# First attention of a two-layer fp32 kernel: one merged score block per head instead of two

## The chip, the cores and the metric

One Trainium2 chip, one of its cores. The metric is device time in microseconds of one execution. Everything is fp32; most matrix products are made of three passes over a high and a low part (hi*hi, hi*lo, lo*hi).

## What is computed

Two transformer mixers follow each other on a sequence of 512 tokens of width 2048. The change lies in the first one, a sliding-window attention with 32 query heads of 64, 4 key/value heads (groups of 8 query heads), a T5 bias and a sink per head:

```python
def swa_sink_mixer(h, w_in, q_gain, k_gain, sinks, rel_table, w_out):
    q, k, v, gate = jnp.split(h @ w_in, [...], axis=-1)          # L = SWA_BLOCK = SWA_WINDOW = 128
    q = rms_norm(q.reshape(bsz, seq, SWA_KV_HEADS, SWA_GROUP, SWA_HEAD_DIM), q_gain)
    k = rms_norm(...); v = ...; k_pad, v_pad = jnp.pad(k, pad), jnp.pad(v, pad)
    dist = qi + L - kj                                           # qi: 0..127, kj: 0..255
    in_band = (dist >= 0) & (dist < SWA_WINDOW)
    def one_block(args):                                         # a block of 128 queries
        s = jnp.einsum('bqhgd,bkhd->bhgqk', qj, kb) * scale + bias
        s = jnp.where(in_band & (start - L + kj >= 0), s, -jnp.inf)
        m = jnp.maximum(jnp.max(s, axis=-1, keepdims=True), sink)
        p = jnp.exp(s - m)
        p = p / (jnp.sum(p, axis=-1, keepdims=True) + jnp.exp(sink - m))
        return jnp.einsum('bhgqk,bkhd->bqhgd', p, vb)
    return (o * jax.nn.silu(gate)) @ w_out
```

A query of a block sees 128 keys out of 256: in the block before its own those with a column above its own, in its own block those up to it. So each of the 128 columns is allowed in exactly one of the two blocks.

## The kernel before, in words

There is no scheduler: each engine's program is written out, and semaphores order them. The first attention runs inside the projections of the first layer. For each key/value head `g` (four) there are 32 half steps `H`. In each, TensorE issues six 512-column matmuls of a projection (two of four token tiles; `project` L744 to L746, or `project_gate` L760 to L762 for the last `g`), and between them pieces of the attention of group `g`. Two half steps use up one k tile of weights, which ScalarE splits into a high part (`make_hi` L1360) and GpSimd into a low part (`make_lo` L1988), three tiles ahead of TensorE, once in every even half step.

The attention of a group has 16 units `u` (4 pairs of heads `hp` by 4 query blocks `j`; n counts over all groups). For unit `u`:

- half step u + 11, TensorE `scores` (L864, L865): for both heads of the pair 128 queries against 256 keys (128 for j = 0), into one PSUM bank per head. It waits for `s_m`, VectorE's signal that it has read the unit before.
- VectorE `soften` in the same half step: copies the sink (L2253), then for each head one custom instruction (L2256) that reads the scores from PSUM, adds the bias, negates, writes `sm` and keeps the extreme value.
- u + 12, ScalarE `weigh` (L1468): the exponential with its sum, 257 columns a head, into `p_w`.
- u + 13, VectorE `denominators` (L2263, L2266): reciprocal, then the rescaling of `p_w`, 512 columns (256 for j = 0). In VectorE's program it stands ahead of the `soften` of that half step.
- u + 14, TensorE `turn_p` (L878): transposes the weights, four 128 x 128 blocks (two for j = 0), after the scores of that half step. ScalarE `keep_pT` (L1478) copies them to SBUF.
- H = 18, 22, 26, 30, TensorE `values` (L891): the product of a pair with `vg`, eight matmuls, between that half step's scores and transposes; VectorE `keep_o` (L2270) copies the result.

ScalarE's order in a half step is `weigh`, the copies of the turned queries, `keep_pT`, and in an even one the weight split. Queries and keys are turned in half steps 3 and 6 to 9 (L853).

Of the kernel before, what the change touches and what calls it, by code (L numbers as in the profile page):

```python
# [127 lines left out]
def build(nc, a, out):  # L128
    with ExitStack() as ctx:
# [30 lines left out]
        p_w = over("p_w", [P, 3, 2, 256 + 1], B_HI + 8192)  # L160
        sm = over("sm", [P, 2, 2, 256 + 1], B_HI + 14368)
# [3 lines left out]
        kT_lo = over("kT_lo", [P, S], B_HI + 28736, F32R)  # L165
        o_T = over("o_T", [P, KC, S], B_LO)
# [18 lines left out]
        den = sb("den", [P, 2, 2])  # L185
# [9 lines left out]
        pT, P_W = place("pT", [P, 2, NT * 256])  # L195
# [150 lines left out]
        s_scaled_p, s_r_row = sem("s_scaled_p"), sem("s_r_row")  # L346
# [210 lines left out]
        def meta_window(unit):  # L557

            return metaT[:, unit:unit + FULL // META].rearrange("p a b -> p (a b)")

# [160 lines left out]
        def _(pe):  # L721
# [113 lines left out]
            for k in range(KC):  # L835
                for t in range(NT):
                    project(1, k, t, setA_hi, setA_lo)
                if k == 12:
                    pe.wait_ge(s_r_row, 1)
                    for t in range(NT):  # L840
                        last = mm(turn[0][:, t * P:(t + 1) * P], ones[:], r_diag[:, t], start=True, stop=True)
                    last.then_inc(s_r_row, 1)

            def q_turn(g, b):

                if b == 0:
                    pe.wait_ge(s_kdup, g + 1)
                else:
# [7 lines left out]
            def scores(g, u):  # L856
# [3 lines left out]
                pe.wait_ge(s_m, g * UNITS + u + EARLY)  # L860
# [7 lines left out]
            def turn_p(g, u):  # L868
# [5 lines left out]
                else:  # L874
                    pe.wait_ge(s_pT, g * UNITS + u)
# [465 lines left out]
        def _(act):  # L1341
# [111 lines left out]
            for k in range(KC):  # L1453
                split_hi(1, k)
                if k == 13:
                    act.wait_ge(s_r_row, 2)
                    nc.scalar.activation(r_row[:], turn[0][:], ACT.Copy).then_inc(s_r_row, 1)
# [3 lines left out]
            def weigh(g, u):  # L1461

                n = g * UNITS + u
                act.wait_ge(s_m, n + 1 + EARLY)
                act.wait_ge(s_tr, n)
                first = P if u % NT == 0 else 0
                for h in range(2):
                    last = nc.scalar.activation(p_w[:, n % 3, h, first:], sm[:, u % 2, h, first:], ACT.Exp,  # L1468
                                                bias=negm[:, u % 2, h:h + 1], scale=-1.0, accum_out=den[:, u % 2, h:h + 1])
                last.then_inc(s_p, 1)  # L1470

            def keep_pT(g, u):
                act.wait_ge(s_tr, g * UNITS + u + 1 + EARLY)
                j = u % NT
                if j == 0:
                    act.wait_ge(s_pv, 4 * g + u // NT + EARLY)
                first = P if j == 0 else 0
                nc.scalar.activation(pT[:, :, j * 256 - P + first:j * 256 + P],  # L1478
                                     turn[0][:].rearrange("p (h k) -> p h k", h=2)[:, :, first:256], ACT.Copy).then_inc(s_pT, 1)
# [12 lines left out]
            for g in range(4):  # L1492
                for H in range(32):
# [12 lines left out]
                    if 0 <= H - 14 < UNITS:  # L1506
                        keep_pT(g, H - 14)
                    if H % 2 == 0:
# [473 lines left out]
        def _(pool):  # L1982
# [50 lines left out]
            root(r_x[:], ss_x[:], NT, ROOT_X)  # L2033
            for k in range(KC):
# [147 lines left out]
        def _(dve):  # L2182
# [32 lines left out]
            last.then_inc(s_r_row, 1)  # L2215
# [31 lines left out]
            def soften(g, u):  # L2247
# [4 lines left out]
                hp, first = u // NT, P if u % NT == 0 else 0  # L2252
                V.tensor_copy(sm[:, u % 2, :, 256:257], sink_g[:, 2 * hp:2 * hp + 2].unsqueeze(2))  # L2253
# [698 lines left out]
```

## Time and profile before

| | |
|---|---|
| median of 3 runs | 1585.67 us (1583.68 to 1586.33) |
| profiled execution | 1584.18 us |
| its span | 1582.3 us |
| TensorE busy | 1569.8 us (99%) |
| VectorE, ScalarE, GpSimd busy | 889.5, 811.2, 675.0 us |
| first attention, from its first turn of keys | 101 us to 363 us |

The span is the time between the first and the last instruction of the program. A matmul's busy time begins with its issue and overlaps that of the next, so the distance between starts tells what one costs TensorE. A long duration of an instruction on VectorE or GpSimd can contain a wait that no semaphore shows.

### The profile page before, as it was taken

To read this page: it belongs to the slowest core of one execution; us is meant where nothing else is said; L and a number is where in the kernel's file an instruction comes from. 1 tells how busy PE (TensorE), PEld (TensorE's weight loads), DVE (VectorE), ACT (ScalarE), POOL (GpSimd) and SP (SyncE) were. 2 spreads that over 40 slices of the span, in tenths; PEclk is the share of its full clock that TensorE was granted. 3 is DMA by queue.
4 is the path that set the end of the run, shared out by engine and by line. 5 is a ranking of instruction groups with operands and counts; after the bars stand their busy time and mean duration, and the time that the engine had idled before them with its cause. 6 is when DMAs were issued, how large, how long until landed. Compare 5 with 4: busy or idle time off the path is not lost.

```text
span 1582.3 us, 22135 instructions
## 1 busy us (share of the span) xinstructions
PE 1569.8 (99%) x8143; PEld 1276.7 (81%) x8143; DVE 889.5 (56%) x1846; ACT 811.2 (51%) x1695; POOL 675.0 (43%) x569
## 2 busy tenths in 40 slices
PE   9999999999999999999999999999999999999998
PEld 7788888888888888887777787888887888888886
DVE  4257757674357876468554532423255454876675
ACT  5456776764334455454444365444466665344561
POOL 5543433436766304575111034544444426664022
PEclk9999999999999999999999999999999999999999
DMA  9554655656887878858999858545554325625762
GB/s 345 146 166 94 163 122 156 161 119 149 192 203 182 241 238 271 222 192 176 258 274 292 198 184 284 168 133 142 160 158 128 114 68 143 151 80 159 241 239 106
DMA packets 139383, 285.41 MB, mean 180 GB/s; under 512 B 11227, under 2 KB 17820, under 8 KB 138604
## 3 DMA queue, kind: packets, MB, share of 16 engines
q1 hardware_dynamic: 85660, 164.49, 31.3%
q0 software_dynamic: 31664, 81.70, 25.1%
q10 hardware_dynamic: 21952, 37.81, 7.6%
q8 instruction: 65, 1.06, 0.3%
q14 instruction: 42, 0.34, 0.1%
HBM read 259.01 MB, written 92.06 MB: 222 GB/s over the span
## 4 chain that ended last, share of the span: by engine, by line
PE 91%; DMA 3%; POOL 2%; ACT 1%; issue 1%; DVE 1%; SPq 0%; POOLq 0%; DVEq 0%
PE acc L744 14%; PE acc L746 14%; PE acc L745 14%; PE acc L760 3%; PE acc L762 3%; PE acc L761 3%; PE turn L1237 3%; PE acc L926 2%; PE acc L927 2%; PE acc L928 2%; PE sc L926 2%; PE turn L926 2%; PE sc L928 2%; PE sc L927 2%; PE turn L927 2%; PE turn L928 2%
## 5 line engine op out<-in xcount | busy, mean ns | idle before, releaser
L1988 POOL TENSOR_TENSOR w_lo<-w_raw,w_hi 128x512 fp32r<-128x512 f32 x341 | 510.1, 1505 | 651.7 <-ACT w_hi L1360 650.8
L1360 ACT ACTIVATE w_hi<-w_raw 128x512 fp32r<-128x512 f32 x565 | 354.1, 629 | 445.5 <-PE acc L746 174.1
L744 PE MATMUL acc<-w_hi,setA_hi 128*128 128x512 f32 (+1 forms) x820 | 331.2, 404 | 0.9 <-ACT stage L1374 0.5
L746 PE MATMUL acc<-w_hi,setA_lo 128*128 128x512 f32 (+1 forms) x820 | 315.9, 385 | 0.0
L745 PE MATMUL acc<-w_lo,setA_hi 128*128 128x512 f32 (+1 forms) x820 | 314.8, 384 | 0.0
L2413 DVE TENSOR_TENSOR w_lo<-w_raw,w_hi 128x512 fp32r<-128x512 f32 x224 | 156.2, 703 | 134.7 <-ACT w_hi L1360 134.0
L746 PEld LDWEIGHTS acc<-w_hi,setA_lo 128*128 128x128 f32 x820 | 153.9, 188 | 31.5
L744 PEld LDWEIGHTS acc<-w_hi,setA_hi 128*128 128x128 f32 x820 | 154.4, 188 | 29.5 <-issue 4.9
L745 PEld LDWEIGHTS acc<-w_lo,setA_hi 128*128 128x128 f32 x820 | 154.7, 189 | 24.1
L760 PE MATMUL acc<-setA_hi,w_hi 128*128 128x512 f32 x256 | 101.9, 398 | 0.0
L762 PE MATMUL acc<-setA_lo,w_hi 128*128 128x512 f32 x256 | 99.9, 390 | 0.0
L761 PE MATMUL acc<-setA_hi,w_lo 128*128 128x512 f32 x256 | 99.7, 389 | 0.0
L744 PE MATMUL acc<-w_hi,setB_hi 128*128 128x512 f32 x192 | 76.5, 398 | 0.3 <-POOL w_lo L1988 0.3
L746 PE MATMUL acc<-w_hi,setB_lo 128*128 128x512 f32 x192 | 75.0, 390 | 0.0
L745 PE MATMUL acc<-w_lo,setB_hi 128*128 128x512 f32 x192 | 74.8, 390 | 0.0
L1468 ACT ACTIVATE p_w<-sm,negm 128x257 f32<-128x257 f32 (+1 forms) x128 | 60.5, 475 | 21.7 <-DVE negm L2256 21.5
L1817 ACT ACTIVATE p<-sm,negm 128x144 f32<-128x144 f32 (+3 forms) x96 | 54.5, 569 | 30.5 <-DVE negm L2731 18.6
L1478 ACT ACTIVATE pT<-turn 128x256 f32<-128x256 f32 (+1 forms) x64 | 34.9, 545 | 42.9 <-PE turn L878 42.8
L762 PEld LDWEIGHTS acc<-setA_lo,w_hi 128*128 128x128 f32 x256 | 48.0, 188 | 10.3
L760 PEld LDWEIGHTS acc<-setA_hi,w_hi 128*128 128x128 f32 x256 | 48.1, 188 | 9.6 <-issue 0.5
L761 PEld LDWEIGHTS acc<-setA_hi,w_lo 128*128 128x128 f32 x256 | 48.1, 188 | 9.1
L2256 DVE CUSTOM_DVE_ANT_0 sm<-sc,bias,sink_g 128x256 f32<-128x256 f32 (+1 forms) x128 | 52.1, 444 | 0.1
(552 smaller groups left out, 3192.0 us busy)
## 6 DMA issues: line engine op xcount, KB each, us to landing
w_raw<-in_swa_w_in SPq DMA_DIRECT2D x35, 1024.0 KB, 7.6
w_raw<-in_w_in SPq DMA_DIRECT2D x32, 1024.0 KB, 5.6
w_raw<-sum_out SPq DMA_DIRECT2D x64, 256.0 KB, 4.5
sum_k<-in_w_in POOLq DMA_DIRECT2D x24, 512.0 KB, 6.6
sum_out<-in_swa_w_out POOLq DMA_DIRECT2D x24, 512.0 KB, 7.5
sum_v<-in_w_in POOLq DMA_DIRECT2D x24, 512.0 KB, 8.7
w_raw<-in_w_in SPq DMA_DIRECT2D x48, 256.0 KB, 5.5
sum_out<-in_w_out POOLq DMA_DIRECT2D x24, 512.0 KB, 6.8
```

The costliest lines, as they stand in the source:

```text
L744: mm(acc[t][:, 0:cols], hi[:, kc, rows], wh, start=(k == 0), stop=False)
L745: mm(acc[t][:, 0:cols], hi[:, kc, rows], wl, start=False, stop=False)
L746: last = mm(acc[t][:, 0:cols], lo[:, kc, rows], wh, start=False, stop=(k == K - 1))
L760: mm(acc[t][:], wh, setA_hi[:, k], start=(k == 0), stop=False)
L761: mm(acc[t][:], wl, setA_hi[:, k], start=False, stop=False)
L762: last = mm(acc[t][:], wh, setA_lo[:, k], start=False, stop=(k == KC - 1))
L926: mm(dst, hi, wh, start=start, stop=False)
L927: mm(dst, hi, wl, start=False, stop=False)
L928: last = mm(dst, lo, wh, start=False, stop=stop)
L1360: nc.scalar.activation(w_at(f)[0], raw_of(f), ACT.Copy).then_inc(done, 1)
L1988: nc.gpsimd.tensor_tensor(lo, raw_of(f), hi.bitcast(F32), ALU.subtract).then_inc(s_lo, 1)
L2413: V.tensor_tensor(lo, raw_of(f), hi.bitcast(F32), ALU.subtract).then_inc(s_wlo, 1)
```

## The change

The two score blocks of a head are merged after the bias: VectorE takes the smaller of the two halves (both are negated, and a banned entry is 1e30), so that exponentials, rescaling, transposes and their copies are 128 columns a head in every unit. In the product, all weights are multiplied with the values of the own block, and those that belong to the block before (columns above the diagonal, `pT_before`, a product with the mask `above`) once more with `v_step`, the difference of the values of the two blocks. The sink copy is made only for the units that begin a buffer's use in a pair (`u % 4 < 2`). `s_m` now counts twice for a unit with j > 0: after the read, which `scores` waits for, and after the `min`, which `weigh` waits for; `softened` and `befores` are these counts. VectorE's `soften` stands ahead of `denominators`, `keep_before` behind it, and `keep_o` is ScalarE's. The semaphore of `r_row` is merged into another.

```diff
+        v_step = over("v_step", [P, NT - 1, HD], B_HI + 30784)
+        def softened(units):
+            return EARLY + 2 * units - (units + NT - 1) // NT
...
             def scores(g, u):
-                pe.wait_ge(s_m, g * UNITS + u + EARLY)
+                n = g * UNITS + u
+                pe.wait_ge(s_m, softened(n - 1) + 1 if n > 0 else EARLY)
...
             def turn_p(g, u):
                 for h in range(2):
-                    for c in range(1 if j == 0 else 0, 2):
-                        last = nc.tensor.transpose(turn[0][:, (2 * h + c) * P:(2 * h + c + 1) * P],
-                                                   p_w[:, n % 3, h, c * P:(c + 1) * P], ident[:])
+                    last = nc.tensor.transpose(turn[0][:, h * P:(h + 1) * P], p_w[:, n % 3, h, 0:P], ident[:])
...
             def values(g, hp):
+                pe.wait_ge(s_before, befores(g * UNITS + (hp + 1) * NT))
-                for c in (0, 2, 1, 3):
-                    keys, end = slice(c * 256, min(c * 256 + 256, 7 * P)), min(c * P + 256, S)
+                for b in range(NT):
                     for h in range(2):
-                        last = mm(o_ps[h * HD:(h + 1) * HD, c * P:end], vg[:, c], pT[:, h, keys],
-                                  start=(c == 0), stop=(c == 3))
+                        last = mm(o_ps[h * HD:(h + 1) * HD, b * P:(b + 1) * P], vg[:, b], pT[:, h, b * P:(b + 1) * P],
+                                  start=(b == 0), stop=False)
+                for b in range(1, NT):
+                    for h in range(2):
+                        last = mm(o_ps[h * HD:(h + 1) * HD, b * P:(b + 1) * P], v_step[:, b - 1], pT_before[:, h, b * P:(b + 1) * P],
+                                  start=False, stop=(b == NT - 1))
...
             def weigh(g, u):
-                act.wait_ge(s_m, n + 1 + EARLY)
+                act.wait_ge(s_m, softened(n + 1))
-                    last = nc.scalar.activation(p_w[:, n % 3, h, first:], sm[:, u % 2, h, first:], ACT.Exp,
+                    last = nc.scalar.activation(p_w[:, n % 3, h], sm[:, u % 2, h], ACT.Exp,
...
+            def keep_o(g, hp):
+                act.wait_ge(s_pv, 4 * g + hp + 1 + EARLY)
+                nc.scalar.activation(o_T[:, 4 * g + hp], o_ps[:], ACT.Copy).then_inc(s_o, 1)
...
             def soften(g, u):
+                if n >= 2:
+                    dve.wait_ge(s_p, n - 1)
+                if n > 0:
+                    dve.wait_ge(s_m, softened(n))
+                if u % NT < 2:
+                    V.tensor_copy(sm[:, u % 2, :, P:P + 1], sink_g[:, 2 * hp:2 * hp + 2].unsqueeze(2))
                 for h in range(2):
                     head = 2 * hp + h
-                    last = V.tensor_tensor_reduce(sm[:, u % 2, h, first:256], sc[h][:, first:256],
+                    dst = s_both[:, h] if first == 0 else sm[:, u % 2, h, 0:P]
+                    last = V.tensor_tensor_reduce(dst, sc[h][:, first:256],
                                                   bias[:, head, first:], -1.0, sink_g[:, head:head + 1],
                                                   ALU.add, ALU.min, negm[:, u % 2, h:h + 1])
                 last.then_inc(s_m, 1)
+                if first == 0:
+                    dve.wait_ge(s_m, softened(n) + 1)
+                    V.tensor_tensor(sm[:, u % 2, :, 0:P], s_both[:, :, 0:P], s_both[:, :, P:256], ALU.min).then_inc(s_m, 1)
...
             def denominators(g, u):
+                rows = p_w[:, (g * UNITS + u) % 3, :, 0:P]
+                V.tensor_tensor(rows, rows, rden[:, u % 2].unsqueeze(2).to_broadcast([P, 2, P]), ALU.mult).then_inc(s_scaled_p, 1)
+            def keep_before(g, u):
+                dve.wait_ge(s_pT, g * UNITS + u + 1)
+                V.tensor_tensor(pT_before[:, :, j * P:(j + 1) * P], pT[:, :, j * P:(j + 1) * P],
+                                above[:].unsqueeze(1).to_broadcast([P, 2, P]), ALU.mult).then_inc(s_before, 1)
...
+                    if 0 <= H - 11 < UNITS:
+                        soften(g, H - 11)
                     if 0 <= H - 13 < UNITS:
                         denominators(g, H - 13)
-                    if 0 <= H - 11 < UNITS:
-                        soften(g, H - 11)
+                    if 0 <= H - 14 < UNITS:
+                        keep_before(g, H - 14)
```

VectorE, half step 16 (scores of unit 5 in `sc`, weights of unit 3 in `p_w`) of a group; ISA is the custom instruction that reads the scores, shown for the first of two heads. Before:

```order
L2263 RECIPROCAL rden<-den 128x2 [waits s_p]
L2266 TENSOR_TENSOR p_w<-p_w,rden 128x2x256 [waits s_d]
L2253 COPY sm<-sink_g 128x2 [waits s_score]
L2256 ISA sm,negm<-sc,bias,sink_g 128x256
L2256 ISA negm 128x1
```

Now:

```order
L2282 COPY sm<-sink_g 128x2 [waits s_m,s_p,s_score]
L2286 ISA s_both,negm<-sc,bias,sink_g 128x256
L2286 ISA negm 128x1
L2292 TENSOR_TENSOR sm<-s_both 128x2x128 [waits s_m]
L2296 RECIPROCAL rden<-den 128x2 [waits s_p]
L2298 TENSOR_TENSOR p_w<-p_w,rden 128x2x128 [waits s_d]
L2307 TENSOR_TENSOR pT_before<-pT,above 128x2x128 [waits s_pT]
```

The rescaling (into `p_w`), which the transposes of the next half step wait for, stood ahead of the reads of the scores; now the two reads and the `min` are ahead of it, and the masked copy (`pT_before`) is behind it.

TensorE, half step 18: transposes of half step 17, then scores of unit 7 and values. Before:

```order
L878 MATMUL turn<-ident,p_w 128x128 [waits s_pT,s_scaled_p]
L878 MATMUL turn<-ident,p_w 128x128 x3
L744 MATMUL acc<-w_hi,setA_hi 128x512 [waits s_lo]
L864 MATMUL sc<-kT_hi,qT_a 128x256 [waits s_m]
L891 MATMUL turn<-pT,vg 64x256 [waits s_o,s_qT,s_pT]
L891 MATMUL turn<-pT,vg 64x256 x5
L891 MATMUL turn<-pT,vg 64x128 x2
```

Now:

```order
L891 MATMUL turn<-ident,p_w 128x128 [waits s_pT,s_scaled_p]
L891 MATMUL turn<-ident,p_w 128x128
L756 MATMUL acc<-w_hi,setA_hi 128x512 [waits s_lo]
L878 MATMUL sc<-kT_hi,qT_a 128x256 [waits s_m]
L903 MATMUL turn<-pT,vg 64x128 [waits s_qT,s_o,s_before,s_pT]
L903 MATMUL turn<-pT,vg 64x128 x7
L907 MATMUL turn<-pT_before,v_step 64x128 x6
```

The transposes are two instead of four, the values fourteen matmuls instead of eight, and their wait has `s_before`, VectorE's masked copy, beside ScalarE's copy.

## Rows read from the trace of the kernel before

**Rows 1.** Busy time and share on the page; engine, us, records.
```profile
PE 1569.8 (99%) x8143; PEld 1276.7 (81%) x8143; DVE 889.5 (56%) x1846; ACT 811.2 (51%) x1695; POOL 675.0 (43%) x569
```

**Rows 2.** All waits of TensorE, first and last of eight: total, times, longest.
```profile
PE sc L808 <- POOL half L2026: 1.7, 1, 1.7
...
PE acc L744 <- POOL w_lo L1988: 0.3, 1, 0.3
```

**Rows 3.** Busy time of each engine in one group of the first attention, 101.14 to 168.38.
```profile
101.14:168.38 67.24, 67.24 (x398) 55.22 (x397) 46.61 (x142) 46.13 (x120) 26.70 (x24) 1.00 0.59 141
```

**Rows 4.** Timeline of TensorE, 187.1 to 196.8 us (start, length).
```profile
187.18 0.28 PE L864 MATMUL sc<-kT_hi,qT_a 128*128 128x256 f32 x1
...
187.66 0.38 PE L878 MATMUL turn<-ident,p_w 128*128 128x128 f32 x2
189.26 0.22 PE L864 MATMUL sc<-kT_hi,qT_a 128*128 128x128 f32 x1
...
191.50 0.28 PE L864 MATMUL sc<-kT_hi,qT_a 128*128 128x256 f32 x1
...
191.85 0.28 PE L865 MATMUL sc<-kT_lo,qT_a 128*128 128x256 f32 x1
191.97 0.60 PE L878 MATMUL turn<-ident,p_w 128*128 128x128 f32 x4
193.78 0.28 PE L864 MATMUL sc<-kT_hi,qT_a 128*128 128x256 f32 x1
...
196.07 0.29 PE L864 MATMUL sc<-kT_hi,qT_a 128*128 128x256 f32 x1
...
196.65 0.44 PE L891 MATMUL turn<-pT,vg 128*64 128x256 f32 x2
```

**Rows 5.** Busy time of L891 alone (records) in two stretches of one product.
```profile
263.93:265.27 1.34, 1.34 (x12) 0.92 (x14) 1.00 0.83 289
265.28:265.55 0.27, 0.27 (x6) 0.14 (x2) 1.00 1.11 417
```

**Rows 6.** Timeline of VectorE after the scores of 191.50 us.
```profile
192.17 0.17 DVE L2253 COPY sm<-sink_g 128x2 f32<-128x2 f32 x1
192.25 0.48 DVE L2256 CUSTOM_DVE_ANT_0 sm<-sc,bias,sink_g 128x256 f32<-128x256 f32 x1
...
193.05 0.17 DVE L2263 RECIPROCAL rden<-den 128x2 f32<-128x2 f32 x1
193.25 0.43 DVE L2266 TENSOR_TENSOR p_w<-p_w,rden 128x256 f32<-128x256 f32 x1
```

**Rows 7.** Weight loads of the transposes (source view): ns min/median/max.
```profile
L878 PEld LDWEIGHTS turn<-ident,p_w x224: 137/140/145, 120.3 to 359.9; 128*128 128x128 f32 x112
```

**Rows 8.** Timeline of ScalarE, 188.1 to 191.8 us.
```profile
188.16 0.39 ACT L1478 ACTIVATE pT<-turn 128x256 f32<-128x256 f32 x1
188.44 0.62 ACT L1360 ACTIVATE w_hi<-w_raw 128x512 fp32r<-128x512 f32 x1
...
191.37 0.41 ACT L1468 ACTIVATE p_w<-sm,negm 128x129 f32<-128x129 f32 x1 [0.46 <-DVE negm L2256]
```

**Rows 9.** Timelines of VectorE and GpSimd, 184.5 to 190.8 us.
```profile
184.55 1.29 POOL L1988 TENSOR_TENSOR w_lo<-w_raw,w_hi 128x512 fp32r<-128x512 f32 x1 [2.21 <-ACT w_hi L1360]
185.22 0.91 DVE L2266 TENSOR_TENSOR p_w<-p_w,rden 128x256 f32<-128x256 f32 x1
...
188.94 0.69 DVE L2266 TENSOR_TENSOR p_w<-p_w,rden 128x512 f32<-128x512 f32 x1
189.14 1.64 POOL L1988 TENSOR_TENSOR w_lo<-w_raw,w_hi 128x512 fp32r<-128x512 f32 x1 [3.30 <-ACT w_hi L1360]
189.85 0.95 DVE L2253 COPY sm<-sink_g 128x2 f32<-128x2 f32 x1 [0.22 <-PE sc L865]
```

**Rows 10.** VectorE by shape, 100 to 370 us: busy us, mean ns.
```profile
L2256 DVE CUSTOM_DVE_ANT_0 sm<-sc,bias,sink_g 128x256 f32<-128x256 f32 x96 | 42.3, 478 | 0.0
...
L2266 DVE TENSOR_TENSOR p_w<-p_w,rden 128x256 f32<-128x256 f32 x16 | 8.8, 548 | 0.5
```

More of the change, by code:

```diff
@@ L158, in build @@
         bias = over("bias", [P, GROUP, 256], B_HI)
-        p_w = over("p_w", [P, 3, 2, 256 + 1], B_HI + 8192)
-        sm = over("sm", [P, 2, 2, 256 + 1], B_HI + 14368)
+        p_w = over("p_w", [P, 3, 2, P + 1], B_HI + 8192)
+        s_both = over("s_both", [P, 2, 256], B_HI + 11328)
+        above = over("above", [P, P], B_HI + 32128)
+        sm = over("sm", [P, 2, 2, P + 1], B_HI + 14368)
         qT_a = over("qT_a", [P, GROUP // 2, S], B_HI + 18496, F32R)
@@ L559, in meta_window, with befores @@
             return metaT[:, unit:unit + FULL // META].rearrange("p a b -> p (a b)")
+        def softened(units):
+            return EARLY + 2 * units - (units + NT - 1) // NT
+        def befores(units):
+            return (NT - 1) * (units // NT) + max(units % NT - 1, 0)
         def head_T(b, h):
@@ L838, in _ @@
                 if k == 12:
-                    pe.wait_ge(s_r_row, 1)
+                    pe.wait_ge(s_rel, 2)
                     for t in range(NT):
                         last = mm(turn[0][:, t * P:(t + 1) * P], ones[:], r_diag[:, t], start=True, stop=True)
-                    last.then_inc(s_r_row, 1)
+                    last.then_inc(s_rel, 1)
             def q_turn(g, b):
@@ L1455, in _ @@
                 if k == 13:
-                    act.wait_ge(s_r_row, 2)
-                    nc.scalar.activation(r_row[:], turn[0][:], ACT.Copy).then_inc(s_r_row, 1)
+                    act.wait_ge(s_rel, 3)
+                    nc.scalar.activation(r_row[:], turn[0][:], ACT.Copy).then_inc(s_rel, 1)
             act.wait_ge(s_kn, 2)
@@ L1507, in _ @@
                         keep_pT(g, H - 14)
+                    if H >= 18 and (H - 18) % NT == 0:
+                        keep_o(g, (H - 18) // NT)
                     if H % 2 == 0:
@@ L2033, in _ @@
             root(r_x[:], ss_x[:], NT, ROOT_X)
+            nc.gpsimd.memset(above[:], 1.0).then_inc(s_ident, 1)
+            pool.wait_ge(s_ident, 4)
+            nc.gpsimd.affine_select(out=above[:], in_=above[:], compare_op=ALU.is_gt, fill=0.0, base=0,
+                                    pattern=[[-1, P]], channel_multiplier=1).then_inc(s_ident, 1)
             for k in range(KC):
@@ L2214, in _ @@
                 last = V.tensor_scalar(r_diag[:, t], ident[:], r_x[:, t:t + 1], None, ALU.mult)
-            last.then_inc(s_r_row, 1)
+            last.then_inc(s_rel, 1)
             dve.wait_ge(s_small, 80)
@@ L2259, in soften @@
                 last.then_inc(s_m, 1)
+                if first == 0:
+                    dve.wait_ge(s_m, softened(n) + 1)
+                    V.tensor_tensor(sm[:, u % 2, :, 0:P], s_both[:, :, 0:P], s_both[:, :, P:256], ALU.min).then_inc(s_m, 1)
             def denominators(g, u):
                 dve.wait_ge(s_p, g * UNITS + u + 1)
[L2263 to L2270 removed]
+                after(dve, V.reciprocal(rden[:, u % 2], den[:, (g * UNITS + u) % 3]))
+                rows = p_w[:, (g * UNITS + u) % 3, :, 0:P]
+                V.tensor_tensor(rows, rows, rden[:, u % 2].unsqueeze(2).to_broadcast([P, 2, P]), ALU.mult).then_inc(s_scaled_p, 1)
+            def keep_before(g, u):
+                j = u % NT
+                if j == 0:
+                    return
+                if j == 1:
+                    dve.wait_ge(s_pv, 4 * g + u // NT + EARLY)
+                dve.wait_ge(s_pT, g * UNITS + u + 1)
+                V.tensor_tensor(pT_before[:, :, j * P:(j + 1) * P], pT[:, :, j * P:(j + 1) * P],
+                                above[:].unsqueeze(1).to_broadcast([P, 2, P]), ALU.mult).then_inc(s_before, 1)
             def keep_gate(c):
```

36 lines of the change are left out of this document (15 added, 21 removed).

## The prediction

> **What bounds the kernel now.** I read the page's busy shares first: TensorE is busy 99% of a 1582.3 us span [rows 1]. Then the waits of TensorE: the longest is 1.7 us at the start, the shortest listed 0.3 us, none of the eight lies in the first attention, and together they are under 5 us [rows 2]. So time here is the sum of what TensorE issues, and a gain must come from it. The table by stage shows the same for one key/value group of the first attention (32 half steps, 67.24 us): TensorE 67.24 us busy, VectorE 46.6, ScalarE 46.1, GpSimd 26.7, granted clock 1.00 (the 2.4 GHz level) [rows 3]. Four groups are four such stretches. VectorE has 20.6 us to spare per group, but it is not evenly spread: with scores and transposes in flight, a half step is 2.28 us long, and in it VectorE works some 1.8 (192.17 to 193.25, and 0.69) [rows 6, 9].
>
> The lengths of half steps come from the timeline of TensorE [rows 4]. Scores to scores is 2.08 us (187.18 to 189.26) where the half step turns two blocks (first block of a pair), and 2.28 and 2.29 us (191.50, 193.78, 196.07) where it turns four. The distance from the transposes' start to the next scores is 1.60 us (187.66 to 189.26) against 1.81 us (191.97 to 193.78).
>
> **The sum, TensorE.** *Transposes.* In 48 of 64 units two of four transposes go: 2.28 or 2.29 less 2.08 is 0.21 us a unit, 48 x 0.21 = 10.1 us. The four records of a unit span 0.60 us and one takes 0.27, so they follow each other every 0.11 us [rows 4]: 96 x 0.11 = 10.6 us is the other bound. I take **-10.2**. The Trainium skill, page "TensorE: Matmul & The Clock Gate", section "Back-to-back issue gap", gives some 81 ns for a 128-column matmul with its weight load in a sustained stream; by it the 96 would be worth only 7.8 us, an estimate. The row measures the fp32 transposes of this kernel, so it decides.
>
> *Values.* Eight matmuls (six of 256 columns, two of 128) become fourteen of 128: 1792 columns either way. The six wide ones (12 records) take 1.34 us, 0.22 each; the two narrow ones take 0.27 us or a little less to the last start, 0.11 to 0.13 each [rows 5]. 14 x 0.11 = 1.54 against 1.56; the six more issues cost at most their own 0.11 each, 0.66 a pair, were they not shorter. I take **+0.5** for all 16 pairs (0 to 10).
>
> **VectorE.** Per unit behind the first block it gains the `min` of two halves (256 elements) and `keep_before` (256), the rescaling shrinks from 512 to 256; the copy of o (0.69 us, 16 times) leaves for ScalarE; half of the sink copies go. The nearest row for each 256-element operation with both inputs in SBUF is the old rescaling of a first block, 0.43 us undisturbed [rows 6]. Counted at the distance to the next start, 0.36, that is 12 x 0.72 more, 12 x 0.27 and 4 x 0.6 less: some +2.5 us in a group. On the average that fits. It is the order that doesn't.
>
> Take t = 0 at the scores of unit 5 (half step 16; it turns unit 2). Last score at 0.64 (191.50 to 191.85 + 0.28) [rows 4], VectorE's sink copy from 0.67, its two reads from 0.75 at 0.40 each (192.25 to 193.05), the last maximum out at 1.64 [rows 6]. The new `min` must wait for VectorE's own signal, 1.67 to 2.10; reciprocal from 2.03, rescaling of unit 3 from 2.23. Before, that rescaling stood *ahead* of the reads. TensorE wants it for the transposes of unit 3 at 2.08 + 0.47 = 2.55. Undisturbed it is there at 2.66 and, with a weight load of 0.14 [rows 7], the transposes start at 2.80: 0.25 late.
>
> It will not be undisturbed. ScalarE copies unit 2's transposes from 0.88 (0.85 their last result, as 187.66 + 0.38), begins the weight tile's high part 0.28 later and needs 0.62, and GpSimd starts its low part 0.08 after that [rows 8]: at 1.86, inside the `min`. What happens then, two pairs of rows show [rows 9]. GpSimd's 1.29 us subtraction, begun at 189.14 while the rescaling ran (188.94 to 189.63), took 1.64: it ran from 0.14 before that ended. A 256-element rescaling begun at 185.22 under GpSimd's (184.55 to 185.84) ended at 186.13, 0.29 after it: 0.91 instead of 0.43. The groups by shape agree: 16 such rescalings have a mean of 548, while the reads of PSUM stay at 478 [rows 10]. So the two engines exclude each other where VectorE reads SBUF twice. The Trainium skill says so too ("SBUF — State Buffer", "Who interferes with whom": the loser waits for the whole instruction), and it speaks against this change, which gives VectorE two such operations more per unit.
>
> Hence GpSimd gets through at 2.10 - 0.14 = 1.96 and ends at 3.25; the rescaling ends at 3.54, the transposes start at 3.68 instead of 2.55: **1.13 us of stall**. GpSimd's window to do so reaches from the reads to 2.23, so its start may be 0.3 later or much earlier. VectorE is now late: `keep_before` of unit 2 from 3.47, reads of unit 6 from 3.83 to 4.72, `min` to 5.18, rescaling to 5.74, `keep_before` of unit 3 to 6.10. TensorE: scores of unit 7 at 3.68 + 1.60 = 5.28, values 0.58 later (196.07 to 196.65) at 5.86 [rows 4], but they need unit 3's masked part: 6.10 + 0.14 = 6.24, **0.38 us**. During the values (1.6 us) VectorE catches up. This is 1.51 us for each pair whose values run among scores: three of four.
>
> Two smaller ones per group. Before the first transposes half steps are 2.08 - 0.21 = 1.87 long; unit 0's rescaling follows unit 2's `min` and ends at 2.58, usable at 2.72, wanted at 2.34: 0.38, with the low part of half step 12 about **0.45**. And after a values step ScalarE copies o before it splits the weights, so that GpSimd's operation starts with the scores of units 8 and 12 and holds the sink copy (0.95 instead of 0.17 in such a case [rows 9]); the next scores are late by about **0.25**, twice. A group: 3 x 1.51 + 0.45 + 0.5 = 5.5; four: **+21.9**. ScalarE's own changes (exponentials 0.41 instead of 0.50 twice a unit [rows 8], copies halved, 0.6 for o) leave it lighter. "Banks freed at the read" frees nothing earlier: the old signal too came with the second read; it only keeps the `min` out of that wait. The mask, the difference of v and the merged semaphores are issued once, or once a group outside the scores, and I put them at nothing; their cover is the lead of three weight tiles, and gone it would cost under 1 us.
>
> Sum: -10.2 + 0.5 + 21.9 = +12.2, rounded to **+12**. The profiled execution took 1584.18 us for its span of 1582.3, so 1596.2 for one like it; against the median of 1585.67 this is 1597.5. Bounds: if the new operations ran at 0.36 a piece, VectorE would be 0.2 us a unit quicker and the stall about 17, +7; if GpSimd comes after the rescaling and holds `keep_before` instead, reads, the next scores and the values are late, about 0.8 + 0.9 a pair, which with slower `min`s of 0.5 makes +16 to +18.
>
> **The rivals.** *A, all of it hidden* (faster): VectorE is 69% busy in the stage, and stalls are absorbed because its engine runs ahead between pairs. Place: the transposes; price: none; it decides if the rescaling lands before 2.41, that is if `min` and its wait cost under 0.2 us together. Then only -10.2 + 0.5: 1576. For it: not one wait of TensorE today [rows 2]. Against it: the operation of this size takes 0.43 [rows 6]. The skill's "Perfetto Trace Analysis", section "Identifying the Most-Contended Engine", would have one cut the busiest engine first, and by occupancy that is TensorE; that rule gives this rival's time. *B, no collision with GpSimd* (no change): the order stalls of 0.25 at the transposes remain, and reckoned on as above 0.40 at the values, 0.65 a pair, with 0.45 a group: 2.4 a group, 9.6 in all, net -0.1: 1585.6. It decides if GpSimd asks outside of 0.75 to 2.23. *C, heavier* (slower): +16 to +18, 1603.
>
> **How the numbers follow.** Forecast 0.62, C 0.08, a milder stall (+4 to +8) 0.04, B 0.15, A 0.11. Slower by over 0.2% (3.2 us, about what a measurement of this kernel can tell from no change) is 0.74; B spreads over both sides of none, 0.11 within 0.2% and 0.04 beyond; so faster is 0.15. The range takes C and B in and leaves A out: 1582 to 1604; the forecast's own is 1592 to 1602.
>
> **What would show it.** Right: in the first attention TensorE waits for VectorE, the longest total before the transposes (`turn`) about 1 us a time, released by the rescaling, 12 times; a second group before the values released by the masked copy, 12 times of some 0.4; 256-element rescalings of over 1 us; a group of about 70 us instead of 67.24, with TensorE busy some 64.7 of it. Wrong: groups of 64.7 us and no such waits (A), or waits of 0.2 to 0.4 alone (B); a values step longer by over 0.1; or a difference outside the first attention, where nothing should move.

## The result, and the profile after

| | before | after |
|---|---|---|
| median on the same chip | 1584.76 us (4 runs) | 1599.7 us (4 runs) |
| profiled span | 1582.3 us | 1597.6 us |
| second group of the first attention, k turn to k turn | 67.25 us | 71.09 us |

The changed kernel is slower: ratio 1.0093, 95% interval 1.0075 to 1.011, that is some 14.7 us. The forecast was 1597.5 with a range of 1582 to 1604. The granted clock was 1.00 in both throughout the first attention. A k turn is the first transpose of a group's keys; from one to the next is a group. Ratios, here and below, are of fast executions alone; one of the eight of the kernel with the paced low part took 5306 us and is not among them.

The page's busy line [rows 1] and TensorE's waits [rows 2] of the changed kernel, matmuls (PE) first, then weight loads (PEld); columns: total us, times, longest:

```profile
PE 1569.3 (98%) x8239; PEld 1275.5 (80%) x8239; DVE 903.5 (57%) x1898; ACT 799.4 (50%) x1711; POOL 676.4 (42%) x571
...
PE turn L891 <- DVE p_w L2298: 11.2, 16, 0.9
PE turn L903 <- issue: 2.7, 12, 0.2
...
PE turn L866 <- DVE kT_lo L2264: 1.1, 3, 0.4
PE acc L756 <- ACT stage L1390: 1.0, 3, 0.4
...
PEld turn L891 <- DVE p_w L2298: 14.5, 16, 1.1
...
PEld turn L903 <- issue: 6.3, 16, 0.4
```

TensorE is as busy as before, 1569.3 against 1569.8 us, in a span 15.3 us longer. It has 96 fewer transposes, and 96 more records all the same, because the values of a pair leave 28 records where they left 16. It now waits 16 times at the transposes (L891) for the rescaling (L2298): 12 times at units 3, 7 and 11 of a group and 4 times at unit 0. It waits 12 times or more at the values (L903), three times at the k/q turns (L866) and three times at the first matmul of a projection, twice at L756 and once at L772. (The third wait in the row of L756, 0.4 us, lies outside the first attention; the kernel before has one like it.) The prediction has neither the waits at the k/q turns nor those at the first matmuls.

The second group, as [rows 3] for the first (us, then busy us and records of PE, PEld, DVE, ACT, POOL, clock, DMA share, GB/s):

```profile
173.00:244.10 71.10, 66.94 (x422) 54.54 (x421) 51.22 (x157) 42.90 (x123) 26.71 (x24) 1.00 0.56 133
```

TensorE was busy in all 67.24 us of a group; now it is busy 66.94 of 71.10, so that 4.2 us are seen as idle. The stalls are longer than that, 6.4 us in the list below, because busy time covers a part of each: a score matmul is recorded as 0.28 us long where the next usually starts 0.12 behind it, so the first 0.16 us of a wait counts as busy, and the pair of transposes behind a stall is itself recorded as longer (0.44 against 0.38).

The turn of unit 3 in the changed kernel, from the timeline of all engines; it answers to [rows 6, 9]:

```profile
198.26 0.62 ACT L1376 ACTIVATE w_hi<-w_raw 128x512 fp32r<-128x512 f32 x1
...
198.76 0.42 DVE L2292 TENSOR_TENSOR sm<-s_both 128x256 f32<-128x256 f32 x1
...
198.96 1.36 POOL L2008 TENSOR_TENSOR w_lo<-w_raw,w_hi 128x512 fp32r<-128x512 f32 x1 [1.81 <-ACT w_hi L1376]
199.10 0.15 DVE L2296 RECIPROCAL rden<-den 128x2 f32<-128x2 f32 x1
...
199.29 1.31 DVE L2298 TENSOR_TENSOR p_w<-p_w,rden 128x256 f32<-128x256 f32 x1
...
199.51 0.28 PE L879 MATMUL sc<-kT_lo,qT_a 128*128 128x256 f32 x1
...
200.53 0.41 DVE L2307 TENSOR_TENSOR pT_before<-pT,above 128x256 f32<-128x256 f32 x1
200.66 0.20 PEld L891 LDWEIGHTS turn<-ident,p_w 128*128 128x128 f32 x2 [1.07 <-DVE p_w L2298]
200.66 0.44 PE L891 MATMUL turn<-ident,p_w 128*128 128x128 f32 x2 [0.87 <-DVE p_w L2298]
```

GpSimd asks at 198.96, inside the `min` (198.76 to 199.18), and is let in. It ends at 200.32. The rescaling, issued at 199.29, ends at 200.60: 0.28 after GpSimd, where undisturbed it takes 0.43. The transposes start 1.15 us after the last score matmul; undisturbed the distance is 0.12 (191.85 to 191.97 [rows 4]). The reciprocal of two numbers ran in between at its usual length.

I laid the starts of TensorE's matmuls side by side for the two kernels, without those of transposes and values. The distance between the traces grows by 14.1 us over the first attention, from 1.3 to 15.4, lies between 14.0 and 15.4 afterwards and ends at 15.3. In the second group it changes in these places: each unit behind the first of a pair takes 0.19 to 0.24 less; units 3, 7 and 11 bring 1.06 to 1.09 of stall each (1.04 to 1.10 in all four groups); each of their values 0.31; unit 0's transposes 0.47, and the scores of unit 3 ahead of them 0.16; the scores of units 9 and 13 0.29 and 0.26; the next projection's first two matmuls 0.53, and the q turn of half step 6 0.55. The last two come three times each, for there are three next projections.

### The profile page after: what moved, and what is told of

Same layout as the page of the kernel before. It is cut to its first block, busy times and chain, and to the rows that moved or that the text cites. A ratio compares the mean times of both kernels' runs of the same rounds, so it can differ in the third digit from the quotient of the medians.

```text
span 1597.6 us, 22483 instructions
## 1 busy us (share of the span) xinstructions
PE 1569.3 (98%) x8239; PEld 1275.5 (80%) x8239; DVE 903.5 (57%) x1898; ACT 799.4 (50%) x1711; POOL 676.4 (42%) x571
## 4 chain that ended last, share of the span: by engine, by line
PE 85%; DVE 6%; DMA 3%; ACT 2%; POOL 2%; issue 2%; SPq 0%; ACTq 0%; DVEq 0%; POOLq 0%
PE acc L756 14%; PE acc L758 13%; PE acc L757 13%; PE acc L772 3%; PE acc L774 3%; PE acc L773 3%; PE turn L1253 3%; PE acc L942 2%; PE acc L943 2%; PE acc L944 2%; PE sc L942 2%; PE turn L942 2%; PE sc L943 2%; PE sc L944 2%; PE turn L944 2%; PE turn L943 2%
## 5 line engine op out<-in xcount | busy, mean ns | idle before, releaser
L756 PE MATMUL acc<-w_hi,setA_hi 128*128 128x512 f32 (+1 forms) x820 | 331.2, 404 | 1.2 <-ACT stage L1390 1.0
L756 PEld LDWEIGHTS acc<-w_hi,setA_hi 128*128 128x128 f32 x820 | 154.3, 188 | 29.8 <-issue 5.8
L772 PE MATMUL acc<-setA_hi,w_hi 128*128 128x512 f32 x256 | 101.8, 398 | 0.3 <-ACT stage L1390 0.3
L756 PE MATMUL acc<-w_hi,setB_hi 128*128 128x512 f32 x192 | 76.2, 397 | 0.0
L1483 ACT ACTIVATE p_w<-sm,negm 128x129 f32<-128x129 f32 x128 | 50.4, 397 | 40.1 <-DVE sm L2292 21.9
L772 PEld LDWEIGHTS acc<-setA_hi,w_hi 128*128 128x128 f32 x256 | 48.1, 188 | 10.0 <-issue 0.9
L2766 DVE MEMSET tick<- 128x1 f32 x96 | 5.7, 59 | 81.1 <-PE sc L1192 67.0
L1253 PE MATMUL turn<-nat_v,pT 128*128 128x128 f32 x320 | 48.8, 283 | 0.4
```

The costliest lines, as they stand in the source:

```text
L756: mm(acc[t][:, 0:cols], hi[:, kc, rows], wh, start=(k == 0), stop=False)
L772: mm(acc[t][:], wh, setA_hi[:, k], start=(k == 0), stop=False)
L1253: mm(dst, pT2[:, u % 2, b * P:(b + 1) * P], nat_v[:, buf, b], start=(b == 0), stop=False)
```

## The experiments

Two claims were open. **One:** the loss is the order of VectorE's queue together with GpSimd's exclusion. **Two,** found in the comparison: 1.07 us a group comes from the output copy on ScalarE. (The expectations split this as 0.45 at the matmul and 0.62 at the turn; by the steps above it is 0.53 and 0.55.) All ratios are to the kernel before, on the same chip. "Group" is the distance from the second to the third k turn (67.25 before, 71.09 after); four times its change is the steadiest measure, for single executions differ by 1.4 us before the attention begins (below); it takes four times what comes three times only.

| kernel | ratio, 95% interval | group, us |
|---|---|---|
| changed kernel | 1.0093, 1.0075 to 1.011 | 71.09 |
| output copy on VectorE | 1.006, 1.0048 to 1.0072 | 69.44 |
| low part paced | 1.0037, 1.0023 to 1.0051 | 69.22 |
| both | 1.0005, 0.9996 to 1.0014 | 67.43 |
| no low parts | 0.9988, 0.9979 to 0.9996 | 67.02 |
| no masked product | 1.0058, 1.0044 to 1.0072 | 70.22 |
| rescaling first | 1.007, 1.0057 to 1.0082 | 70.31 |
| min last, copy on VectorE | 1.005, 1.0038 to 1.0063 | 69.18 |
| the same, low part paced | 0.9969, 0.9958 to 0.9981 | 65.91 |
| before, copy on ScalarE | 1.002, 1.0011 to 1.0028 | 68.49 |
| before, reads first | 1.0006, 0.9997 to 1.0015 | 67.55 |
| before, low part paced | 1.001, 1.0001 to 1.0018 | 67.43 |

**The low part paced.**

```diff
                     if H % 2 == 0:
+                        if H >= 14:
+                            pool.wait_ge(s_scaled_p, g * UNITS + min(H - 13, UNITS - 1) + 1)
                         split_lo(2 + g, H // 2)
```

> The changed kernel with one wait added on GpSimd: from half step 14 on, its low part of the weights starts only after the rescaling of the same half step. Theory one (GpSimd gets the shared access at the end of the min, holds it for its 1.3 us, and the rescaling waits for it): the stalls at the turns of units 3, 7 and 11, 12 of about 1.1 us, fall to 0.3 or less each; the values wait may grow by 0.2 each, since the masked product now meets the low part. Time falls by 9 us (6 to 12) against the changed kernel, to about 1590. Rival (VectorE is late through the order and the amount of its own work; GpSimd is not in it): the stalls stay near 1.1 us, the time within 2 us of the changed kernel, or slower, since weights come up to 3 us later.

Measured: 1.0037 against 1.0093, 8.9 us less. Nothing but GpSimd's start was moved. TensorE's waits in 90 to 315 us (three groups' turns):

```profile
PE turn L903 <- issue: 3.5, 9, 0.4
PE turn L891 <- DVE p_w L2300: 0.8, 3, 0.3
...
PEld turn L903 <- issue: 6.2, 12, 0.6
...
PEld turn L891 <- DVE p_w L2300: 2.9, 12, 0.5
```

The 1.1 us stalls at the turns are gone. What is left there is unit 0, as before, and 0.12 us at each of units 3, 7 and 11: their transposes start 0.24 behind the last score matmul instead of 0.12. The values wait longer: they start 0.67 behind the last score matmul where it was 0.51, and their weight loads wait up to 0.6 us where it was 0.4. That is not mainly for the reason I gave: the low part now meets the next unit's `min` (mean 515 ns against 472; the masked product 446 against 430), and the masked product stands behind that. The rival falls.

**No low parts at all.**

```diff
-                        split_lo(2 + g, H // 2)
+                        f = B[2 + g] + H // 2 + AHEAD
+                        pool.wait_ge(s_hi, number[f] + 1)
+                        nc.gpsimd.memset(w_at(f)[1].bitcast(F32), 0.0).then_inc(s_lo, 1)
```

> The changed kernel with GpSimd's subtraction for the low parts of the weights in the four projections beside the first attention replaced by a write of zeros of the same size at the same place in its queue: the low parts of these weights are left out of the computation, the matmuls on them stay. Theory one (two engines exclude each other while GpSimd reads and writes for 1.3 us): VectorE's rescalings of over 1 us are gone, the turn stalls fall from about 1.1 to 0.2 us, time 10 to 14 us under the changed kernel, unless a pure write excludes as well; then each is as long as the write, and the gain is 1.3 minus that length, times 12. Rival (VectorE's own order): no change within 2 us.

Measured: 0.9988, 16.6 us less than the changed kernel, above the 10 to 14 expected. In the second group the turns of units 3, 7 and 11 give back 0.87 each. The rest comes from other places: unit 0's transposes 0.13, the scores of units 3, 9 and 13 0.17, 0.29 and 0.25, and the q turn of half step 6 0.53. The values still start 0.50 behind the last score matmul. This kernel still has the copy on ScalarE, and is already 0.1% ahead of before. So the stalls at the scores of units 9 and 13 and at that q turn need GpSimd's subtraction as well as the copy: at the q turn VectorE's four scalings of q take 2.50 us together beside the write and 3.59 beside the subtraction. Only the 0.53 at the next projection stays here, and comes from the copy alone. VectorE and GpSimd by shape, 100 to 370 us (busy us, mean ns, idle before):

```profile
L2300 DVE TENSOR_TENSOR p_w<-p_w,rden 128x256 f32<-128x256 f32 x64 | 27.3, 426 | 2.2
L2294 DVE TENSOR_TENSOR sm<-s_both 128x256 f32<-128x256 f32 x48 | 20.4, 425 | 1.7
...
L2068 POOL MEMSET w_lo<- 128x512 f32 x63 | 33.2, 526 | 211.0 <-ACT w_hi L1376 211.0
```

and one such step from its timeline:

```profile
194.60 0.42 DVE L2294 TENSOR_TENSOR sm<-s_both 128x256 f32<-128x256 f32 x1
...
194.78 0.53 POOL L2068 MEMSET w_lo<- 128x512 f32 x1 [2.69 <-ACT w_hi L1376]
...
195.13 0.42 DVE L2300 TENSOR_TENSOR p_w<-p_w,rden 128x256 f32<-128x256 f32 x1
```

The write from 194.78 to 195.31 lies over the end of the `min` and the start of the rescaling, and neither is longer for it. In the changed kernel the same two groups are:

```profile
L2298 DVE TENSOR_TENSOR p_w<-p_w,rden 128x256 f32<-128x256 f32 x61 | 36.6, 600 | 2.1
L2292 DVE TENSOR_TENSOR sm<-s_both 128x256 f32<-128x256 f32 x48 | 22.7, 472 | 1.7
```

**The output copy back on VectorE.**

The call leaves ScalarE's loop and stands at the end of VectorE's half step:

```diff
-                act.wait_ge(s_pv, 4 * g + hp + 1 + EARLY)
-                nc.scalar.activation(o_T[:, 4 * g + hp], o_ps[:], ACT.Copy).then_inc(s_o, 1)
...
+                dve.wait_ge(s_pv, 4 * g + hp + 1 + EARLY)
+                V.tensor_copy(o_T[:, 4 * g + hp], o_ps[:]).then_inc(s_o, 1)
```

> The changed kernel with the copy of the output (keep_o) back on VectorE, at the end of its half step as before; all else of the change stays. Laid side by side, the traces of before and after show 1.07 us in each of the first three groups that no term of the forecast holds: 0.45 at the first matmul of the next projection and 0.62 at the q turns of half step 6. Theory one (the copy on ScalarE waits for the values, and the evacuation of the next projection's banks stands behind it in ScalarE's queue): both go, and the time falls by about 3.2 us (2 to 4.5) against the changed kernel, with the 12 stalls of about 1.1 us at the turns of units 3, 7 and 11 unchanged. Rival (they come from VectorE's own added work at the head of a group, the differences of the values, or from nothing that this copy touches): no change within 1 us, or up to 3 us slower, because VectorE gets 16 copies of 0.69 us (row of before) back.

Measured: 1.006, 5.2 us less than the changed kernel, where 3.2 (2 to 4.5) was expected. The turn stalls are as they were (11.0 us, 12 times, longest 1.1, at the weight loads in 90 to 315 us), the waits at L866 for `kT_lo` and at L756 for `stage` are gone, and so are those of the scores of units 9 and 13: 0.25 to 0.29 twice a group, 2.1 us in four. These the prediction has as a term that comes from this very copy, and I left them out of what I expected here. 3.2 + 2.1 is 5.3. ScalarE's timeline at the end of a projection, changed kernel:

```profile
162.54 0.38 ACT L1492 ACTIVATE pT<-turn 128x256 f32<-128x256 f32 x1 [0.71 <-PE turn L891]
165.60 0.60 ACT L1497 ACTIVATE o_T<-turn 128x512 f32<-128x512 f32 x1 [2.68 <-PE turn L907]
166.09 0.62 ACT L1376 ACTIVATE w_hi<-w_raw 128x512 fp32r<-128x512 f32 x1
166.62 2.42 ACT L1390 ACTIVATE stage<-acc,r_x 128x512 f32<-128x512 f32 x4
```

and with the copy on VectorE:

```profile
160.86 0.39 ACT L1492 ACTIVATE pT<-turn 128x256 f32<-128x256 f32 x1 [0.71 <-PE turn L891]
161.14 0.62 ACT L1376 ACTIVATE w_hi<-w_raw 128x512 fp32r<-128x512 f32 x1
161.67 1.28 ACT L1390 ACTIVATE stage<-acc,r_x 128x512 f32<-128x512 f32 x2
```

ScalarE stood idle for 2.68 us in front of `o_T`, waiting for the values, with the weight split and the evacuation behind it in its queue. From the last copy of `pT` to the evacuation it is 4.08 us in the one and 0.81 in the other.

**The same part alone, in the kernel before.** Edit: `keep_o` taken from VectorE and put behind `keep_pT` on ScalarE.

> The kernel before with one part of the change alone: the copy of the output moved from VectorE to ScalarE, behind the copy of the turned scores. Theory one (it delays the evacuation of the next projection by waiting for the values): 1 us in each of the first three groups, so +3 us (1.5 to 4.5), in the gaps at the first matmul of each projection and at the q turns. Rival (before, ScalarE's queue had other slack and VectorE gains 16 times 0.69 us): within 1 us of before, or up to 4 us faster.

Measured: 1.002 (1.0011 to 1.0028), +3.2 us, though VectorE is 9 us less busy (880.1 against 889.5). The group is 1.24 us longer, and the same two steps are in it, 0.54 at the next projection and 0.52 at the q turn. Theory two holds in both directions.

**Both repairs together.**

> The changed kernel with both repairs and its order kept (score reads, min, rescaling, masked product): the output copy on VectorE, and GpSimd's low part behind the rescaling of its half step from half step 14 on. By themselves they gave back about 5.2 and 8.9 us of the 14.7. Theory one (two separate causes, so they add, and little else is lost): 1.000 to 1.002 times before, 1586 to 1588, with the change's own gain of some 10 us still eaten by waits at the values (the masked product now meets the low part) and at each group's first turn. Rival (they overlap, or one hides the other): the ratio stays at 1.003 or above; or, if GpSimd was all, the order is nothing and it comes to 0.997, as with the min last.

Measured: 1.0005, 13.9 us less than the changed kernel, where 5.2 and 8.9 add to 14.1. The two repairs add. (They touch different stalls, since the pacing begins at half step 14 and does nothing at the q turn of half step 6.) What eats the rest of the gain stands in the waits (90 to 315 us):

```profile
PE turn L903 <- issue: 3.5, 9, 0.4
PE turn L891 <- DVE p_w L2294: 0.8, 3, 0.3
PEld turn L903 <- issue: 6.1, 12, 0.6
PEld turn L891 <- DVE p_w L2294: 3.0, 12, 0.5
```

**The masked product left out.** Edit: no `keep_before`, no wait for it, and the second part of the values reads `pT`.

> The changed kernel without the masked product: VectorE's 48 of 0.42 us a piece and the values' wait for them are left out, and the second part of the values multiplies the unmasked scores, so the causal part of the output is not computed. Theory one (it sits behind the rescaling at the end of VectorE's queue and delays only the values of its half step): the turn stalls stay at 12 times 1.1 us, the values' stall of about 0.4 us goes where it was not the matmuls' own start, so 1.5 to 5 us less than the changed kernel, 1594 to 1598. Rival (VectorE's amount of work is what counts, so 20 us less of it frees the turns too): 10 us less or more.

Measured: 1.0058, 5.5 us less by the two ratios (2 to 9 with their intervals) and 3.5 us by the group, 4 x 0.87. The turn stalls stay, 10.9 us in 12 weight loads, longest 1.1, as in the changed kernel. So 48 operations fewer on VectorE, 20 us of its work, don't touch the turns; the amount of its work is not the cause. 0.87 over three values is 0.29 each, which is the values' wait: they start 0.21 us behind the last score matmul here, as before the change, against 0.51 in the changed kernel. The profile itself puts the waits at L903 down to "issue" and doesn't name the masked product; this run does.

**VectorE's old order in the merged kernel.** Edit: `denominators` ahead of `soften`.

> The changed kernel with VectorE's order as before: the rescaling (denominators) ahead of the score reads and the min, all else of the change kept. Theory one (VectorE's queue in a half step is what TensorE waits for, so order only chooses who waits): the 1.1 us at the turns of units 3, 7 and 11 go, and waits come at the scores of units 3, 5 and 7, for the reads now stand behind the rescaling and the low part that may be in front of it: 0.4 to 0.8 us each; against the changed kernel 0 to 4 us less, 1596 to 1600. Rival (reads first is the cause of the loss; the merged form would do well in the old order): 8 us or more less, to 1591 or under.

Measured: 1.007, 3.6 us less than the changed kernel. The stalls moved from the turns to the scores: 0.3 us each at units 3 and 5, and 0.8 each at units 7, 11 and 15, of which I had named only 7 (90 to 315 us):

```profile
PE sc L878 <- DVE negm L2286: 6.1, 12, 0.6
...
PEld sc L878 <- DVE negm L2286: 15.5, 21, 1.1
```

**The kernel before with reads first.** Edit: `soften` ahead of `denominators`, a third slot of `den`, and a wait of the reads for the exponentials two units back.

> The kernel before with one part of the change alone: VectorE's score reads ahead of the rescaling in each half step (with three slots for the denominators in place of two, and one wait for the softened unit two back); both column blocks, their four transposes and all else as before. Theory one (the order costs only together with the min that follows the reads): the reads take 0.81 us of a half step of 2.1 us in front of the rescaling, and the four transposes are still in time or late by up to 0.2 us at one unit in four: 0 to +3 us. Rival (reads first delays the rescaling by itself enough for the turns to stall): 12 stalls of 0.5 us or more, +6 us or more.

Measured: 1.0006, its interval holds no change; the group is 0.3 us longer. Reads first costs next to nothing without the `min`.

**Another place for the min.** Edit: output copy on VectorE; the `min` moved behind the masked product.

```diff
                     if 0 <= H - 14 < UNITS:
                         keep_before(g, H - 14)
+                    if 0 <= H - 11 < UNITS:
+                        merge(g, H - 11)
```

> The same without the wait on GpSimd: output copy on VectorE, order reads, rescaling, masked product, min. Theory one: GpSimd starts its 1.3 us as soon as ScalarE's high part is there, in every second half step, at a place that no longer is the end of the min; where it still gets ahead of one of VectorE's operations on two tensors, that one is late by 0.5 to 1 us, now mostly in front of the min, so that the next unit's reads, and the scores of units 7, 11 and 15 behind them, wait: 12 stalls of 0.4 to 0.8 us, 6 to 10 us above the paced form, about at before (1580 to 1592). Rival (the place of the min alone decides, GpSimd does not): as fast as the paced form within 1.5 us.

and the same with GpSimd's low part behind the masked product (`pool.wait_ge(s_before, ...)` from half step 16 on):

> Three edits to the changed kernel together: the output copy back on VectorE; VectorE's order in a half step is score reads, rescaling, masked product, and the min last; GpSimd's low part waits, from half step 16 on, for the masked product of its half step. The products of the change are all kept. Theory one (order and exclusion are all that the change loses): the stalls of 1.1 us at the turns, of about 0.4 us at the values and those of the output copy all but go, and what is left is the change's own gain, 48 units at 0.21 us less 0.5 us for the values: 10 us under the kernel before, less what remains at a few scores and at each group's first turn (1 to 4 us); 6 to 9 us under before, about 1578. Rival (the merged form needs more of VectorE than a half step has, wherever its parts stand): the stalls come back at the scores of units 5, 7, 9, which wait for the reads, and the time is at or above before.

Measured: 1.005 and 0.9969. Unpaced, GpSimd caught the masked product instead of the rescaling (VectorE and GpSimd, timeline):

```profile
197.26 0.43 DVE L2295 TENSOR_TENSOR p_w<-p_w,rden 128x256 f32<-128x256 f32 x1
197.39 1.44 POOL L2002 TENSOR_TENSOR w_lo<-w_raw,w_hi 128x512 fp32r<-128x512 f32 x1 [1.76 <-ACT w_hi L1376]
...
197.60 1.51 DVE L2304 TENSOR_TENSOR pT_before<-pT,above 128x256 f32<-128x256 f32 x1
```

The masked product ends at 199.11, 0.28 after GpSimd, the `min` behind it late, the next unit's reads late, and the scores after that wait. I had expected 0.4 to 0.8 us for each of those 12 stalls. Their distance to the matmul ahead is 1.15 us (200.58) instead of 0.23, so 0.92 each, and pacing was worth 12.8 us instead of 6 to 10. Paced, these are all of TensorE's waits for another engine in the three groups:

```profile
PE sc L878 <- DVE negm L2282: 0.8, 3, 0.3
...
PEld sc L878 <- DVE negm L2282: 3.0, 6, 0.7
```

This version beats both kernels: 4.9 us under before (interval 3.0 to 6.7), 20 us under the changed one. I had expected 6 to 9. The group gained 1.34 us of the 12 x 0.21 = 2.5 that the transposes give. Of the missing 1.2, the values start 0.17 later each (0.35 to 0.40 behind the last score instead of 0.21), the scores of unit 5 0.41 later (0.64 instead of 0.23), and the values themselves take 0.02 longer. That names 1.0 of it.

**The wait alone, in the kernel before.**

> The kernel before with the wait of GpSimd alone: its low part behind the rescaling from half step 14 on. Theory one (the kernel before has the rescaling ahead of the reads, TensorE waits nowhere for it by more than 0.1 us, so there is nothing for the wait to give back): within 1.5 us of before. Rival (the exclusion costs the kernel before as well, and the faster version owes its time to the wait rather than to the merged block): 3 us faster or more.

Measured: 1.001 (1.0001 to 1.0018), +1.6 us, the group 0.2 longer. The wait gives the kernel before nothing; the gain needs both the merged block and the pacing.

## Why the prediction was right

**Transposes, -10.2.** Right. The steps between the aligned traces are 0.19 to 0.24 a unit, 0.21 forecast. The 81 ns of the Trainium skill, page "TensorE: Matmul & The Clock Gate", section "Back-to-back issue gap", would have made it 0.16 a unit; the rows before were the better guide.

**Values, +0.5.** Sixteen records take 1.66 us from first start to what follows, twenty-eight take 1.68: +0.3 for 16 pairs.

**Turns, 1.13 each.** In the prediction's terms 0.98 to 1.04: the transposes of units 3, 7 and 11 start 1.10 to 1.16 behind the last score matmul instead of 0.12, and 0.06 more is lost in the matmuls behind them. In the second group the low part starts 1.87 after the scores (1.96 forecast) and the rescaling ends at 3.51 (3.54), but the transposes follow it by 0.06 and not by the 0.14 of a weight load. The mechanism is shown: it disappears when GpSimd starts later, when GpSimd only writes, and not when VectorE has 20 us less to do. The Trainium skill's page "SBUF — State Buffer" ("Who interferes with whom") states this exclusion, and the timeline agrees: GpSimd starts 0.22 before the `min`'s recorded end, and the rescaling it holds up ends 0.28 after its own.

**Values' wait, 0.38 each.** Right in kind, somewhat large: 0.29 by the group without the masked product.

**Unit 0, 0.45 a group.** Measured 0.47; its last score stands 0.53 ahead of the transposes instead of 0.12. The scores of unit 3 in the same half step are late by another 0.16, which the sum lacks; that too goes when GpSimd only writes.

**Scores after values, 0.25 twice a group.** Measured 0.25 to 0.29, and the cause is as given: the copy of o stands in front of ScalarE's weight split, and so shifts GpSimd's subtraction. Moving the copy back removes them, and so does leaving the subtraction out.

**What failed.** The weak sentence is "ScalarE's own changes ... leave it lighter". ScalarE is lighter, 799.4 against 811.2 us, but that was taken to cost nothing. It counted the copy's 0.6 us and not what is queued behind its wait. At the last pair of a group the copy waits 2.68 us for the values, the evacuation of the next projection's four banks waits behind it, and with it the first matmul (0.53) and, through the squares and the scaled q, which then run beside GpSimd's subtraction, the turn of half step 6 (0.55). That is 1.07 in three groups, 3.2 us that the sum lacked, and it is why the result lies above the forecast: 12.2 + 3.2 is 15.4, against 14.7 measured; the values' wait, 0.29 instead of 0.38 at twelve places, takes back 1.1. I had looked behind the same copy at units 8 and 12, where GpSimd waits, and not at the one place where TensorE does. The expected sign "nothing should move outside the first attention" held; the expected group "of about 70 us" was 71.1 for this reason. TensorE's busy time in it, 66.94, is not the 64.7 that the prediction gave as a sign: recorded busy time covers a part of each stall. The base of the forecast is also a little loose: 1585.67 and 12 make 1597.7, not 1597.5.

**Rival B** (the order alone, 0.65 a pair) is close to what both repairs together gave: 1.0005, with 0.46 at each of the values (0.67 behind the last score instead of 0.21) and little at the turns. It gave no change, as priced. **Rival A** would have needed an order that nobody waits for; the `min` last, paced, comes near it, at 1.1 us a group above.

## What to carry to other kernels

An operation moved to a less busy engine brings its wait with it: list what stands behind it in that engine's queue at every place, the last one of a loop above all, and who waits for that. Here 0.6 us of work on an engine that was busy 50% cost 5 us, and 3 in the kernel before; a part of that cost arose because the late queue pushed other work beside GpSimd's subtraction. Where two engines exclude each other, the length of the other engine's operation is the price of being caught, and where that operation has slack (here weights three tiles ahead), one wait that places it in a gap was worth more (8.9 us) than the short operations' reordering without it (3.6 us for the rescaling first, 1.6 for the `min` last).

## What was not expected of the hardware

- A write without a read on GpSimd (128x512, 0.53 us) doesn't hold up VectorE's operations on two tensors: 0.42 us with it and without it, where GpSimd's subtraction of two tensors made the same rescaling 1.31. The write is also shorter, but it overlaps two operations and neither is longer. The expectation had left open which way this would go. Whether one read alone would exclude was not tried.
- VectorE's copy of two numbers a partition is held up like the large ones: 1.17 us with the `min` last (at 193.64) under a low part that began at 193.49, against 0.17 [rows 6]. The prediction had the like of it, 0.95 in [rows 9].
- Single executions differ before the attention begins. The first k turn comes at 101.0 to 101.5 us in before and five of the other kernels, and at 102.4 to 102.9 in the other seven, without regard to their edits. The changed kernel and before issue the same matmuls there, and four records of one loop start take:

```profile
5.80 2.08 PE L830 MATMUL acc<-w_hi,setA_hi 128*128 128x512 f32 x4 [0.72 <-ACT w_hi L1446]
```

